# Index keys with index queries, router with its gate, stacked rows, a split routing chain: one change to a two-block transformer kernel

## What is computed

```python
for i in range(2):                                   # first block
    h = x @ w_in[i]        # -> dq dk dv (512 each) sq sk sv (512 each) iq (512) ik (64) iw (8) ga gb (1024 each)
    ya = diff_attention(dq, dk, dv, lam(diff_lambda[i]))
    yb = dsa_attention(sq, sk, sv, iq, ik, iw, topk=64)       # iq, ik, iw rank the keys of each query
    mix = (sigmoid(ga) * (ya @ w_bd) + sigmoid(gb) * (yb @ w_bs)) @ w_out[i]
    x = layer_norm(ALPHA * x + mix, ln1_g[i], ln1_b[i])
    g_prob = softmax(x @ w_route_group[i] + b_rg)             # 4 groups, top 1
    e_prob = softmax((x @ w_route_expert[i] + b_re)[group])   # 8 experts in the group, top 2
    ffn = sum over 32 experts of comb * (silu(x @ w_g) * (x @ w_u)) @ w_d
    ple = sigmoid(x @ w_ple_gate[i]) * (p[i] @ w_ple[i])
    x = layer_norm(ALPHA * x + ffn + ple, ln2_g[i], ln2_b[i])
x = second_block(x, ...)                             # MLA, MOBA, retention, squared-relu MLP; rms_norm at the end
```

## Time and profile before

| what | us |
| --- | --- |
| median of 3 runs | 2069.28 |
| the runs | 2066.51, 2069.28, 2075.98 |
| the profiled execution | 2075.21 |
| its span from the first to the last instruction | 2073.4 |
| mean granted clock of TensorE | 0.96 |

### The profile page before, as it was taken

The page is one execution under the profiler, slowest core; times in us unless marked ns, Lnnn a source line. Parts: engine busy times, 40 slices in busy tenths (PEclk is TensorE's granted clock), DMA queues, the critical chain, the costliest instruction groups (busy, mean ns, idle before and its releaser), DMA issues.

```text
span 2073.4 us, 31189 instructions
## 1 busy us (share of the span) xinstructions
PE 1964.5 (95%) x12616; PEld 1782.3 (86%) x12616; DVE 1408.3 (68%) x2285; ACT 1074.5 (52%) x1667; POOL 84.4 (4%) x86
## 2 busy tenths in 40 slices
PE   7899999999989999999999699999999899999998
PEld 6789879999878898799998589998999789998997
DVE  4866768888658766688886656676444666675444
ACT  4444457677534544577775354444444454444443
POOL 1000010000010000100000100000100000001001
PEclk9999889999889998899999799999999999999999
DMA  6426239999624262399996153344555443354552
GB/s 251 152 82 230 83 122 421 383 406 420 263 103 144 106 233 76 148 408 387 407 420 251 54 198 125 125 161 153 193 184 188 139 157 143 123 183 152 194 183 82
DMA packets 60152, 426.65 MB, mean 206 GB/s; under 512 B 6849, under 2 KB 7233, under 8 KB 9440
## 3 DMA queue, kind: packets, MB, share of 16 engines
q1 hardware_dynamic: 59040, 421.65, 53.8%
q0 software_dynamic: 384, 1.72, 0.3%
q10 hardware_dynamic: 576, 1.19, 0.2%
HBM read 423.49 MB, written 1.05 MB: 205 GB/s over the span
## 4 chain that ended last, share of the span: by engine, by line
PE 84%; DVE 10%; ACT 3%; issue 1%; POOL 1%; DMA 0%; DVEq 0%; POOLq 0%; ACTq 0%; SPq 0%
PE bank L997 68%; PE scp L997 11%; DVE WSl L1361 3%; PE bank L1100 1%; PE bank L1235 1%; ACT WSh L1891 1%; ACT SC L1928 1%; PE bank L1127 1%; PE bank L1085 1%; POOL sm L2114 1%; PE bank L1255 1%; DVE sm L1499 1%; DVE scp L1497 0%; DVE TMP L1484 0%; DVE sm L1322 0%
## 5 line engine op out<-in xcount | busy, mean ns | idle before, releaser
L1361 DVE TENSOR_TENSOR WSl<-ring,WSh 128x1024 fp32r<-128x1024 f32 (+3 forms) x508 | 586.5, 1198 | 227.1 <-ACT WSh L1891 226.0
L1891 ACT CAST WSh<-ring 128x1024 fp32r<-128x1024 f32 (+3 forms) x508 | 496.8, 1031 | 212.4 <-PE bank L997 121.4
L997 PE MATMUL bank<-XTh,WSh 128*128 128x256 f32 x1216 | 349.6, 288 | 7.2 <-DVE A L1534 4.4
L997 PE MATMUL bank<-XTl,WSh 128*128 128x256 f32 x1216 | 346.2, 285 | 0.0
L997 PE MATMUL bank<-XTh,WSl 128*128 128x256 f32 x1216 | 346.1, 285 | 0.0
L997 PE MATMUL bank<-WSh,FA 128*128 128x512 f32 (+1 forms) x848 | 301.5, 389 | 2.7 <-DVE FA L1788 2.6
L997 PE MATMUL bank<-WSl,FA 128*128 128x512 f32 (+1 forms) x680 | 262.5, 386 | 0.0
L997 PEld LDWEIGHTS bank<-XTh,WSh 128*128 128x128 f32 x1216 | 235.6, 194 | 9.2 <-issue 5.5
L997 PE MATMUL bank<-WSh,XTh 128*128 128x512 f32 (+4 forms) x576 | 226.9, 394 | 15.3 <-DVE WSl L1361 12.4
L997 PEld LDWEIGHTS bank<-XTl,WSh 128*128 128x128 f32 x1216 | 235.5, 194 | 0.2
L997 PEld LDWEIGHTS bank<-XTh,WSl 128*128 128x128 f32 x1216 | 235.4, 194 | 0.0
(11 more groups left out here) (271 smaller groups left out, 2932.1 us busy)
## 6 DMA issues: line engine op xcount, KB each, us to landing
ring<-wts SPq DMA_DIRECT2D x270, 1024.0 KB, 4.9
V<-wts SPq DMA_DIRECT2D x42, 1024.0 KB, 12.2
PT<-wts SPq DMA_DIRECT2D x32, 1024.0 KB, 8.7
H<-wts SPq DMA_DIRECT2D x28, 1024.0 KB, 9.5
GT<-wts SPq DMA_DIRECT2D x12, 1024.0 KB, 13.1
A<-wts SPq DMA_DIRECT2D x10, 1024.0 KB, 4.9
ring<-wts SPq DMA_DIRECT2D x4, 832.0 KB, 7.5
ring<-wts SPq DMA_DIRECT2D x2, 768.0 KB, 5.3
```

Of the source, the lines that this page charges most:

```text
L997: return nc.tensor.matmul(dst, lhsT, rhs, start=start, stop=stop)
L1361: nc.vector.tensor_tensor(lo[:, c], buf[:, c], hi[:, c].bitcast(F32), ALU.subtract).then_inc(*lo_done.inc(("block", i)))
L1891: nc.scalar.copy(hi[:, c], buffers[s.buffer][:, c]).then_inc(*hi_done.inc(("half", i, k)))
```

## The change

- **Index.** iq, ik and iw (584 columns) are one product in two parts of IQ = 292 columns: 96 matmuls of 292 columns in four blocks of 1168 columns per partition, instead of 48 of 512 and 48 of 72 in three. ACT writes the second part out in three pieces. `late_loads` waits for an earlier product.
- **Router.** Its 36 columns stand ahead of w_ple_gate's in `parts`: 356, 352 and 352 columns, six blocks, instead of one of 36 and two of 512 (five blocks). `router` follows the first part, for each token tile from its own bank; the tanh of that part waits for DVE's read of the logits. x_hi and x_lo (the split of H for the gather) move ahead of the routing.
- **Rows.** The rows are loaded twice, on partitions 0 to 63 and 64 to 127, and made fp32r: high part above, low part below (`rows`). `spread` is one fp32r matmul per 256 columns over all 128 partitions, with the selector PICK that has a one in both halves.
- **Routing chain.** ROUTE_ORDER, what the expert choice needs, runs before `ranks`; ROUTE_LATE, the values of the two experts, and `kept` (positions, masks) run after the gather's fourth K piece.
- **Norm transposes.** The transposes and their splits stand among `ple` and its copies; p is in OHT, so XT is free earlier; G (also in OHT) waits for the read of w_ple.

```diff
+ROUTE_ORDER, ROUTE_LATE, ROUTE_ACT = (*range(8), *range(10, 22), 26, 28), (8, 9, 22, 23, 24, 25, 27), (3, 14)
+PARTS = [(0, 320), (320, 352), (672, 352)]
+IQ = 292
+    def parts(self, l, c):
+        u, (c0, n) = [], PARTS[c]
+        names = [("w_ple_gate", c0, c0 + n)]
+        if c == 0:
+            names = [("w_route_group", 0, NG), ("w_route_expert", 0, NE)] + names
+        def block(h):
+            i = self.take(*((name, (l,), k, 1, a, b) for k in range(4 * h, 4 * h + 4) for name, a, b in names))
...
+            self.add("wide", name="ple_gate", l=l, c=c, h=h, n=sum(b - a for _, a, b in names), i=i, u=u, src=("ln1", l))
+            self.release(i)
+            if c == 0 and h:
+                self.add("router", l=l, u=u)
...
-        self.columns("w_in", "iq", l, W1["iq"], 512, src)
+        for c in range(2):
+            for f in self.wide("w_in", "iq", l, c, W1["iq"] + IQ * c, IQ, src):
+                f()
...
-        self.tok("ik", l, 0, ("w_in", (l,), 0, KD, W1["ik"], W1["ga"]), 72, src=src)
...
+        if l == 0:
+            self.add("rows")
         self.add("lambda", l=l, u=self.bank("dve"))
...
-        for c in range(4):
-            self.add("ple", l=l, c=c, i=i, u=self.bank("act"), gt=gt)
...
+        for c in range(3):
+            ple(c)
+        xt = self.use("XT", "pe")
+        ple_out(0)
+        ple_out(1)
+        t0 = self.turn_steps("ln1", l, 4, xt=xt)
+        for f in t0[0:2]:
+            f()
+        ple(3)
...
-        i = self.take(*((name, (l,), k, 1, 0, n) for k in range(KD) for name, n in (("w_route_group", NG), ("w_route_expert", NE))))
-        self.add("router", l=l, i=i, u=self.bank("dve"))
-        self.spare.extend(("route", dict(l=l, t=t, n=n)) for n in range(ROUTE_STEPS) for t in range(T))
...
-        blocks = [f for c in range(2) for f in self.wide("w_ple_gate", "ple_gate", l, c, 512 * c, 512, ("ln1", l))]
-        for c, self.lead in enumerate((14, 20, 28, 0)):
...
+        blocks = [f for c in range(3) for f in self.parts(l, c)]
+        xs = self.use("FA", "pe")
+        for c, self.lead in enumerate((0, 0, 12, 18, 18, 0)):
+            if c == 4:
                 self.first("YA", "YB")
+            if c == 5:
                 self.add("ranks", l=l, u=self.bank("dve"))
+            blocks[c]()
+            if c == 0:
+                self.add("x_hi", l=l, fa=xs)
                 self.add("x_lo", l=l)
             if c == 1:
+                self.spare.extend(("route", dict(l=l, t=t, n=n)) for n in ROUTE_ORDER for t in range(T))
...
+            if k == 3:
+                for n in ROUTE_LATE:
+                    for t in range(T):
+                        self.add("route", l=l, t=t, n=n)
+                self.add("kept", l=l)
...
             def spread(dst, name, l, c0, n):
-                m = 4 * len(ROWS)
+                pe.wait_ge(dve_done, "rows")
                 for c in range(c0, c0 + n, 256):
                     r, w = 4 * ROWS.index((name, l)) + c // 256, min(256, c0 + n - c)
-                    last = mm(dst[:, c - c0:c - c0 + w], ident[0:m, r:r + 1].broadcast_to([m, P]), PR[0:m, 0:w], True, True)
+                    last = mm(dst[:, c - c0:c - c0 + w], PICK[:, r:r + 1].broadcast_to([P, P]), PR[:, 0:w], True, True)
...
+                elif s.kind == "rows":
+                    m = 4 * len(ROWS)
+                    nc.vector.tensor_tensor(PICK[:, :], ident[:, 0:m], ident[:, 64:64 + m], ALU.add).then_inc(*dve_done.inc())
+                    dve.wait_ge(act_done, "rows")
+                    nc.vector.tensor_tensor(PR[64:128, :], RAW[64:128, :], PR[64:128, :].bitcast(F32), ALU.subtract).then_inc(
...
+                        dve.wait_ge(pe_done, "read", i)
                         nc.vector.tensor_scalar(G[:, t, :], iota, slot[:, 0, t:t + 1], None, ALU.is_equal).then_inc(*dve_done.inc())
...
+                        if s.c == 0:
+                            act.wait_ge(dve_done, "router", l, t)
```

163 lines of the change are left out of this document (83 added, 80 removed).

## The result

The changed kernel took 2039.05 us, the median of four runs (2033.11 to 2041.4), against 2069.04 for the kernel before: ratio 0.9837, interval 0.9818 to 0.9856. Since single comparisons of these two kernels came out between 0.981 and 0.984, I pooled the runs of this study at its end: 2035.7 is the median of 14 runs of the changed kernel, these four among them, and 2072.8 that of the 44 runs of the kernel before in the later comparisons (2072.6 with the four of this one), a gain of some 37 us. The forecast was 2021.7, from 2009 to 2035. So the sign was right and the size was not: 2039.05 stands 4 us above the range, the pooled median 0.7. The profiled execution took 2033.11 (span 2031.3).

A forecast was written before the change was run, and what follows sets the result against it. PE (95% busy) was taken as the bound, the expert stage as bound to its first H fetch. Terms 8.4 + 12.4 + 13.0 + 9.0 + 4.8 = 47.6 us, off 2069.3, gave 2021.7 us, range 2009 to 2035.

The forecast's parts named there:

- Start: Layer 0 up to ple: index stage 5.1 us earlier, sq 2.8 shorter, lambda's spread 0.5; sum 8.4 us.
- both gate stages: Norm 1 to the first H fetch: fetch earlier by 12.4 us in layer 0 and 13.0 in layer 1.
- Rival 3: New 292- and 352-wide blocks hold the half clock throughout: 56.8 us lost, 2078.5 us; chance 0.03 with other misses that size.
- Rival 2: A better clock: MK at 269, no slow piece in part 0, expert stages lose idle PE time; 2010 us, chance 0.11.
- the 12.4: Layer 0, norm 1 to expert stage: H fetched 12.3 to 14.3 us earlier, less one half-clock piece; bounds 6 and 14.3.
- the transposes among the products: Norm 1: with ple products among the transposes, part 0 starts near 248.3 and logits come at 256.1 instead of 261.05.
- the layer boundary: Between layers: cheaper spreads, shorter index stage and sq at full clock gain 9.0 us, or 6.5 if sq keeps its slow part.
- PE waits 2 us: Layer 1's third index block: its split stands on DVE behind an affine ending at 591.1 and needs 1.44 us.
- Rival 4: Merged blocks split too late everywhere, so PE waits as long as it saves; some 2 us a place, chance 0.02.
- iq starts at 584.0 instead of 586.88: Layer boundary: eight spreads cost PE 0.96 us, or 1.7 at half clock, instead of 3.96, so layer 1's index stage starts earlier.
- sq at 21.8: sq's 96 matmuls at 0.227 each take 21.8 us, from 24.64 in layer 0 and 24.19 in layer 1.
- Rival 1: Part of the gain is given back by slow pieces of sq and gate stages: gain 34.4 us, 2034.9 us; chance 0.24.

The follow-up runs named there:

- turns_apart: The changed kernel with the norm transposes and their splits put back behind all four ple products: 2033.11 us, ratio 0.9811.
- pool_late: The changed kernel with POOL's scaling of X waiting for ACT's last copy of sq: 2040.51 us, ratio 0.9844.
- no_scale: The changed kernel without POOL's scaling of X, its factor taken into w_out's product and norm 1's epsilon: 2034.12 us, repeated 2027.83 us.
- rows_only: The kernel before with only the rows part of the change (rows loaded twice, fp32r spreads with PICK): 2065.82 us, ratio 0.9961.
- best: The changed kernel without POOL's scaling, norm 2's affine moved behind sq's first part, and rows one sq part earlier: 2028.9 us, ratio 0.979.

## Why the prediction was right and wrong

**Right: the widths and what they buy.** 0.135 and 0.160 a step stood as interpolated. Start (7.6 for 8.4), both gate stages (11.7 and 13.8 for 12.4 and 13.0) and norm 2 (5.0 for 4.8) came as summed, and the wait for MK (2.99 in layer 0, 1.68 in layer 1) lies within the 1.3 to 3.4 that the queue of DVE gave. The expert stage followed its first H fetch: 261 to 265 us in every trace, whenever the fetch came. Rival 3, new widths that hold the half clock, fell: part 0 ran at 1.00. Rival 2 fell too. Part 0 had no slow piece, as it asked, but MK did not come early (ranks 32.6 us behind `ple`, which is 270.7 on the time base of the earlier trace rows), and the expert stages got no shorter.

One sum was made loosely and came out all the same: the 12.4 is 13.7 - 1.3, but the middle of 12.3 and 14.3 is 13.3, and a half-clock piece was priced at 1.7. That would be 11.6, and 11.7 was measured.

**Right in the whole, wrong in its reason: the transposes among the products.** I had them start part 0 early, which they do, and counted the gain through the logits. turns_apart shows that the same H fetch comes without them within 0.5 us. That the stage's sum held is therefore in part luck.

**Wrong: the layer boundary, 9.0 forecast, 3.7 measured.** The step that failed is the wait of PE for the third index block. By the three steps of the forecast:
- "PE waits 2 us", then "the last two blocks end at 592.5 + 6.5". From iq to sq I had 15.0, a gain of 3.6. It took 18.6 and 18.8 before, and 19.20, 20.45 and 20.45 after, a loss of 1.3: 4.9 of the 5.3 that the term missed. The wait was seen at the right place and for the right queue, DVE behind its affine, but sized by 1.44 for the two subtractions. They took 4.88, because I had looked at the queue of DVE only, and not at what POOL does at that moment: `scale_x` waits for the same affine, so in after both start at the same time. The wait was 4.51 to 4.83, and the two blocks behind it took 7.8 to 9.0 at clock 0.82 to 0.69 where I had 6.5. Without POOL beside it (pool_late and both no_scale kernels) the same stretch takes 14.5: the sum was right but for the hold. Rival 4 had named this place, and priced it at 2 us.
- "iq starts at 584.0 instead of 586.88", a gain of 2.9. From the first transpose to iq: 7.42 and 10.70 before, 7.70, 7.20 and 7.12 after. Against the trace that the forecast was made from that is almost nothing, by the means it is 1.7. The new spreads take 1.85 at half clock, as priced, but the transposes have a hole of 1.7 to 2.5 in which PE waited for nothing that the profile shows. It stands in all traces with the new spreads, rows_only included (1.80), and in neither of the two without. In best, where the spreads stand behind the first part of sq, it is there too (2.29), so their place does not make it. The row part brings it; by what, is open. The 10.70 is the second trace of before, whose old spreads fell on the half clock:

```profile
578.30:585.42 7.12, 7.12 (x18) 5.17 (x17) 4.21 (x6) 2.31 (x5) 0.00 (x0) 0.50 0.00 0
```

- sq at 21.8: measured 21.81, 21.76 and 21.81.

**Wrong: which execution the sum was made against.** The boundary alone would have left the forecast in its range: 2021.7 + 5.3 = 2027.0. I took the terms from the profiled execution of before, 2075.21 at clock 0.960, and took their sum off the median of three, 2069.28. But the pooled mean of before is 2072.5, 3.2 above that median. And both profiled executions of before took longer than this mean (2075.21 and 2076.28, by 3.3), while the three of after took less than theirs (2033.11, 2036.5 and 2034.57 at 0.973, 0.968 and 0.971; pooled mean 2036.0, by 1.3). So the traces show 3.3 + 1.3 = 4.6 more gain than the runs have, by definition the distance of 41.1 and 36.5. With the 6.5 by which the traces fall short of 47.6, these make 6.5 + 4.6 + 3.2 = 14.3 between 2021.7 and 2036.0, and chance in the four runs of the first comparison the other 3 to 2039.05. In which terms of the forecast the 4.6 sit is open. Not in sq: its slow part, which I counted as the kernel's own, is in all four traces that have the 72-wide products (23.6 to 24.6 us in layer 0, 23.4 to 24.2 in layer 1) and in none of after (22.0 and 21.8). The run times fall as the granted clock rises, which fits a difference made by the clock; no experiment isolates it.

Rival 1, "part of the gain is given back", comes near the right time (2034.9) by luck. It priced slow pieces of sq and of the gate stages, but both sq stages ran at full clock, and the gate stages together gave nothing back (25.5 for 25.4). Its remark on new gaps of 2 to 3 us at the boundary carried no price. The give-back was a new wait and a hole.

## What to carry to other kernels

When a step of one engine is moved to an earlier time, look at what the other engines start at that moment, not only at its own queue: two instructions that never met before may meet then, and the same event may release both. A narrow product that rides in a wider one is safely priced by interpolating between two measured widths. A wait that vanishes is worth what the next chain leaves of it: here a removed wait of 1.5 us was worth nothing, and so was PE's being 2 us earlier at part 0, while taking out POOL's instruction, which I had not put on the critical path, was worth 6. And a sum of terms read from one execution should be taken off the time of that execution, and be given the scatter of the runs.
